# Main attention of a hybrid decoder step: the gate over the row sum goes into the rows of probabilities before they are turned, both branches add up in one PSUM bank

## The reference, cut to what matters

```python
def masked_softmax(s, mask):
    s = jnp.where(mask, s, NEG_INF)
    p = jnp.where(mask, jnp.exp(s - jnp.max(s, axis=-1, keepdims=True)), 0.0)
    return p / jnp.maximum(jnp.sum(p, axis=-1, keepdims=True), TINY)
...
    p = masked_softmax(s, (dist_s >= 0)[:, :, None])
    o_slc = jnp.einsum('bgrqk,bgqkd->bqgrd', p, vg.astype(F32))
...
    o_win = window_prompt(q, k_win, v_win, slopes)
...
    o_nsa = gate[:, :, 0, :, :, None] * o_cmp + gate[:, :, 1, :, :, None] * o_slc + gate[:, :, 2, :, :, None] * o_win
```

## Time and profile before

| | |
|---|---|
| median of 3 runs | 1355.48 us (1353.26 to 1357.56) |
| profiled execution: its span, the one time recorded of it | 1354.8 us |
| PE busy | 1298.8 us (96%) |
| DVE / ACT / POOL busy | 619.4 / 621.8 / 145.7 us |
| main attention, first scores to last spread | about 382 to 1004 us of the span |

### The profile page before, as it was taken

One profiled execution on the slowest core, in us unless ns is written; L12 is line 12 of the kernel. 1 busy time (PEld: TensorE's weight loads), 2 busy tenths in 40 slices (PEclk: granted clock), 3 DMA queues, 4 the chain that ended last, 5 costly groups with the idle time before them and its releaser, 6 DMA issues.

```text
span 1354.8 us, 23612 instructions
## 1 busy us (share of the span) xinstructions
PE 1298.8 (96%) x9533; PEld 1170.1 (86%) x9533; DVE 619.4 (46%) x1387; ACT 621.8 (46%) x1072; POOL 145.7 (11%) x184
## 2 busy tenths in 40 slices
PE   5999998999999999999999999999988989999998
PEld 4999998999988889989888889888866779999876
DVE  6211145645834343433323333466578767453342
ACT  6211336542555536666556645665467542221121
POOL 2100001103300000000000300313010260000000
PEclk9999999999999999999999999999999999899999
DMA  7251453522422211122212221554345656452331
GB/s 207 63 171 42 120 149 103 147 69 61 79 69 59 64 59 60 48 79 64 65 59 79 60 59 52 172 168 147 101 155 197 245 180 193 136 157 64 109 121 59
DMA packets 156908, 145.27 MB, mean 107 GB/s; under 512 B 27360, under 2 KB 141360, under 8 KB 156736
## 3 DMA queue, kind: packets, MB, share of 16 engines
q1 hardware_dynamic: 154016, 135.33, 33.1%
q0 software_dynamic: 2784, 8.43, 2.1%
HBM read 105.88 MB, written 41.88 MB: 109 GB/s over the span
## 4 chain that ended last, share of the span: by engine, by line
PE 56%; ACT 2%; DVE 2%; issue 1%; SPq 0%; DMA 0%; another core or an unknown queue 0%; POOL 0%; DVEq 0%; ACTq 0%
PE ps L240 31%; PE ps L2536 7%; PE ps L1645 4%; PE ps L1679 4%; PE ps L1661 3%; PE ps L1694 1%; PE ps L2443 1%; PE ps L2411 1%; DVE S L2648 1%; PE ps L2447 1%; PE ps L1764 1%; PE ps L2544 1%; PE ps L2502 0%; DMA m_raw<-in_w_branch_a 0%; SPq L3012 0%
## 5 line engine op out<-in xcount | busy, mean ns | idle before, releaser
L240 PE MATMUL ps<-hH,wH 128*128 128x352 f32 (+1 forms) x1320 | 440.0, 333 | 5.8 <-DVE stg L375 3.0
L240 PE MATMUL ps<-hH,wL 128*128 128x352 f32 (+1 forms) x1320 | 425.3, 322 | 0.0
L240 PE MATMUL ps<-hL,wH 128*128 128x352 f32 (+1 forms) x1320 | 424.8, 322 | 0.0
L240 PEld LDWEIGHTS ps<-hH,wH 128*128 128x128 f32 (+1 forms) x1320 | 248.1, 188 | 32.9 <-issue 26.5
L240 PEld LDWEIGHTS ps<-hL,wH 128*128 128x128 f32 (+1 forms) x1320 | 249.1, 189 | 2.2 <-issue 1.9
L240 PEld LDWEIGHTS ps<-hH,wL 128*128 128x128 f32 (+1 forms) x1320 | 247.8, 188 | 0.3
L227 DVE TENSOR_TENSOR wL<-w_raw,wH 128x1024 fp32r<-128x1024 f32 (+1 forms) x70 | 87.8, 1254 | 132.8 <-ACT wH L219 132.7
L2002 DVE CUSTOM_DVE_ANT_0 sP<-ps,dist,stat 128x256 f32<-128x256 f32 (+3 forms) x116 | 58.6, 542 | 176.8 <-issue 108.2
L360 ACT ACTIVATE stg<-ps 128x352 f32<-128x352 f32 x132 | 61.1, 463 | 119.1 <-PE ps L240 117.3
L219 ACT ACTIVATE wH<-w_raw 128x1024 fp32r<-128x1024 f32 (+1 forms) x70 | 73.5, 1050 | 70.5 <-issue 39.5
L2199 ACT ACTIVATE pPT<-ps 128x512 f32<-128x512 f32 x74 | 44.1, 596 | 131.9 <-PE ps L1661 131.8
(11 more groups left out here) (391 smaller groups left out, 2035.1 us busy)
## 6 DMA issues: line engine op xcount, KB each, us to landing
w_raw<-in_w_in SPq DMA_DIRECT2D x61, 512.0 KB, 4.1
p_spill<-stg SPq DMA_DIRECT2D x132, 176.0 KB, 1.8
zt<-p_spill SPq DMA_DIRECT2D x24, 528.0 KB, 4.8
w_raw<-in_w_in SPq DMA_DIRECT2D x17, 256.0 KB, 3.8
gvT<-p_spill SPq DMA_DIRECT2D x8, 528.0 KB, 5.4
x_all<-in_x_prompt SPq DMA_DIRECT2D x8, 512.0 KB, 10.0
m_raw<-in_w_branch_b SPq DMA_DIRECT2D x8, 512.0 KB, 5.5
xr<-in_x_prompt SPq DMA_DIRECT2D x8, 512.0 KB, 3.5
```

Source lines behind the costliest of these rows:

```text
L240: mm = nc.tensor.matmul(ps[0:t.m, bank, 0:NF], w[:, c % 2, t.m * k:t.m * k + t.m], x[n][:, k, :], start=(k == 0 and i == 0), stop=(k == t. ...
```

## The change

The weights go into the rows of probabilities instead of the outputs. For each row, DVE takes max and reciprocal of the two row sums, and then multiplies the whole row of `sP` in place, once for each group, with 1 / row sum and with the gate (one instruction with two factors that are columns of one value per partition). PE's turns wait for that (`weighed`) instead of for the exponentials. Since both branches then come out weighted, they add up in the same 256 columns. The spread on PE, its copy on ACT and the two additions on POOL are gone; DVE's `drain` adds 256 columns of PSUM to `oTn`. ACT's exponentials of the first 49 steps run one cut further ahead.

```diff
             def transposes(m):
...
-                    pe.wait_ge(sem("probs"), 2 * cuts[m][-1][0] + g + 1)
+                    pe.wait_ge(sem("weighed"), 2 * cuts[m][-1][0] + g + 1)
...
-                    col = P * (2 * br + i % 2)
+                    col = P * (i % 2)
...
-                                start=c + k == 0, stop=c + k == blocks_of[n] - 1)
+                                start=br == 0 and c + k == 0, stop=br == 1 and c + k == blocks_of[n] - 1)
...
                 slot(t, 3)
-                for j in closed(m - 1):
-                    spread(j)
...
+            def weigh(m):
+
+                nonlocal weighed
+                while weighed < len(U) and (last_cut(weighed) <= m + LA - 2 or cut_of[weighed, 0] <= m):
+                    n = weighed
+                    r, i, br = U[n]
+                    j = n // 4
+                    dve.wait_ge(sem("probs"), 2 * n + 2)
+                    l, w = lcol[:, j % 2, :, br, i % 2], wcol[:, j % 2, :, br, i % 2]
                     link(nc.vector.tensor_scalar(w, l, TINY, None, ALU.max))
                     link(nc.vector.reciprocal(w, w))
+                    for g in range(G):
+                        p = sP[:, g, P * spot[n]:P * (spot[n] + blocks_of[n])]
+                        col = 8 * (br + 1) + R * g + r
+                        nc.vector.tensor_scalar(p, p, wcol[:, j % 2, g, br, i % 2:i % 2 + 1], gate[:, i, col:col + 1],
+                                                ALU.mult, ALU.mult).then_inc(sem("weighed"), 1)
+                    weighed += 1
...
             def drain(j):
...
-                nc.vector.tensor_tensor(tmp[:, j % 2, :], tmp[:, j % 2, :], ps[:, 6 + j % 2, :], ALU.mult)\
-                    .then_inc(sem("O_out"), 1)
+                o = oTn[:, r, 2 * P * ip:2 * P * ip + 2 * P]
+                nc.vector.tensor_tensor(o, o, ps[:, 6 + j % 2, 0:2 * P], ALU.add).then_inc(sem("O_out"), 1)
...
             def tail_step(m):
 
                 t = m - M0
+                weigh(m)
                 slot(t, 0)
...
             for m in range(ncut):
                 if m >= M0:
                     tail_step(m)
                     continue
+                weigh(m)
                 dve_units(dve, units_at(m) - 1)
...
-            def spread(j):
-
-                act.wait_ge(sem("w_spread"), j + 1)
-                if j >= 2:
-                    act.wait_ge(sem("o_added"), j - 1)
-                copy(tmp[:, j % 2, :], ps[:, 4, :]).then_inc(sem("w_copied"), 1)
...
-                while rows < len(U) and (last_cut(rows) <= m + LA - (1 if m >= M0 else 2) or cut_of[rows, 0] <= m):
+                while rows < len(U) and (last_cut(rows) <= m + LA - 1 or cut_of[rows, 0] <= m):
```

More of the change, by code:

```diff
@@ L1110, in closed @@
             return [j for j in range(4 * R) if last_cut(4 * j + 3) == m]
-        def spread_before(m):
-            return sum(last_cut(4 * j + 3) + 1 < m for j in range(4 * R))
         def units_at(m):
@@ L1484, in turned @@
             act.wait_ge(sem("gv_done"), NV * h + p + 1)
-            if h == 0 and j < 2:
-                act.wait_ge(sem("o_added"), 4 * R - 1 + j)
-            elif h == 0:
+            if h == 0 and j >= 2:
                 act.wait_ge(sem("av_done"), ncut)
@@ L1890, in _ @@
             pool.wait_ge(sem("cmp_out"), PT)
-            add(0)
+            pool.wait_ge(sem("O_out"), 1)
             for name in cmp_sems:
                 pool.sem_clear(sem(name))
-            for j in range(1, 4 * R - 6):
-                add(j)
             first_biases()
-            add(4 * R - 6)
             pool.wait_ge(sem("u_done"), NE)
@@ L2015, in copies @@
                         drain(j)
-            def weigh(j):
-                r, ip = divmod(j, 4)
-                if j >= 2:
[L2021 to L2024, removed]
+            weighed = 0
+            def weigh(m):
[6 more added lines that the diff above has]
+                    l, w = lcol[:, j % 2, :, br, i % 2], wcol[:, j % 2, :, br, i % 2]
                     link(nc.vector.tensor_scalar(w, l, TINY, None, ALU.max))
                     link(nc.vector.reciprocal(w, w))
[L2027 to L2031, removed]
+                    for g in range(G):
[4 more added lines that the diff above has]
+                    weighed += 1
             def drain(j):
-                dve.wait_ge(sem("w_copied"), j + 1)
+                r, ip = divmod(j, 4)
+                if j == 0:
+                    dve.wait_ge(sem("cmp_out"), PT)
                 dve.wait_ge(sem("av_done"), last_cut(4 * j + 3) + 1)
-                nc.vector.tensor_tensor(tmp[:, j % 2, :], tmp[:, j % 2, :], ps[:, 6 + j % 2, :], ALU.mult)\
-                    .then_inc(sem("O_out"), 1)
+                o = oTn[:, r, 2 * P * ip:2 * P * ip + 2 * P]
+                nc.vector.tensor_tensor(o, o, ps[:, 6 + j % 2, 0:2 * P], ALU.add).then_inc(sem("O_out"), 1)
             def decode_queries():
@@ L2240, in probs @@
                 if n % 4 == 0 and j >= 2:
-                    act.wait_ge(sem("w_ready"), j - 1)
+                    act.wait_ge(sem("weighed"), 8 * (j - 1))
                 act.wait_ge(sem("scored"), 2 * (last_part[n] + 1))
@@ L2320, in _ @@
                 act_units(act, units_at(m) - 1)
-                copies(m)
+                pT_copy(m)
                 act_units(act)
```

37 lines of the change are left out of this document (3 added, 34 removed).

## The result

The changed kernel takes 1359.85 us (median of 11 runs, 1358.27 to 1364.01) against 1354.92 us (1350.22 to 1357.56): ratio 1.0033, interval 1.0021 to 1.0044. Run again in a second series it took 1359.70 us against 1355.43 us, ratio 1.0028 (1.0015 to 1.0040). So it is slower by 4 to 5 us. The forecast was 1354.6 us and no measurable change.

A forecast was written before the change was run, and what follows sets the result against it. PE's list was taken to bound the main attention; -16.5 (spreads) + 16.4 (waits) + 1.9 (weight loads) + 1.3 (slow clock) - 2.5 - 1.1 - 0.4 = -0.9 us, so 1354.6 us, with a range of 1347 to 1366.

The forecast's parts named there:

- PE's list bounds the stretch, and the spreads are worth 16.5 us: Main attention: PE busy 615.5 of 626 us; removing 16 spreads of 1.03 us takes 16.5 us off its list.
- The price of a weighing: On DVE: 0.52 ns a column, 347 ns for one weighing of 128 columns.
- The rival of full rate: DVE weighs at 1.04 ns a column, PE waits in twice as many steps: about +13, 1368 us; chance 0.16.
- The waits on the weighing: PE's turns in the main attention wait for DVE's weighed rows: 17 waits, 16.4 us in all.
- The first kind: Rows over three cuts ending a one-unit step (steps 13, 26, 46): PE waits 1.65 us each, 5.3 us in all.
- the third: Steps from 49 on, one unit each, `head_part` ahead of the weighing: 3.0 us in steps 51, 54, 55, 57, 58.
- The rival that the cover holds: DVE reaches the weighings earlier, only step 64's wait and slow clock remain: about 1345 us; chance 0.12.
- The rival of ACT holding up the units' banks: Earlier exponentials delay ACT's bank-freeing copies; PE waits in a quarter of 27 two-unit steps: +6, 1361 us; chance 0.06.
- What hangs on the waits: Behind each of 17 waits PE loads weights for 0.11 us, 1.9 us; clock effects were also counted here.
- the zb wait: PE's 2.6 us wait on a DVE product shrinks by 1.2 us and loses its 1.3 us of slow clock: -2.5.
- The clock: Slow clock costs 1.3 us more behind step 64's wait; 1.3 us of it goes behind the 2.6 us product wait.
- POOL's end: At the very end POOL's last additions hold the next stage's buffers; their removal gives -0.4 us.

The follow-up runs named there:

- Without weighing: The changed kernel with no weighing issued, PE's turns waiting for the exponentials, row sums and gates left out of the output: 1336.09 us, ratio to before 0.9846.
- the third profile of before: The kernel before the change, unedited, run and profiled a third time: 1356.34 us, ratio 1.0005, 602.12 us to cut 64.
- the filled wait: The changed kernel plus 44 additional matmuls on PE that keep it at work during its 5.5 us wait at cut 64: 1357.19 us, ratio to before 1.0016.
- the last row early: The changed kernel with the last row's weighing moved ahead in step 63, before the next stage's factors on DVE: 1355.90 us, ratio to before 1.0005.

## Why the prediction was wrong, step by step

- **PE's list bounds the stretch, and the spreads are worth 16.5 us: right, but for the last one.** The 15 spreads up to cut 64 are 15.4 us of PE. Without weighing 19.3 us go; the forecast for the same terms was 16.5 + 2.5, but 2.0 us of the 19.3 are waits that neither the forecast nor the expectation had (above).
- **The price of a weighing: right**, 344 and 810 ns. The rival of full rate is out.
- **The waits on the weighing: right in place, and in total with some luck.** 16.1 us forecast as 16.4. Steps 13, 26, 46: 1.44, 1.75, 0.95 us (1.65 each; the rows it was worked out from give 1.57); 0, 15, 40, 42: 0.75, 0.80, 0.58, 0.27 (0.85, 0.9, 0.6, 0.3); 51, 54, 55, 57, 58: 4.1 together (3.0); 64: 5.50 (5.5). The first kind came 0.8 us below, the third 1.1 above. The forecast counted 17 waits; its own list has 13 places, and 13 is what the trace shows. The rival that the cover holds is out in this order, and comes true as soon as the order is changed. The rival of ACT holding up the units' banks is out too: PE waits for no copy of a unit by ACT.
- **"What hangs on the waits": the step that failed.** It had 1.9 us of weight loads behind the waits and no more. Against the third profile of before, the stretch to cut 64 is 3.5 us longer, and neither profile has slow clock in a busy part of it. 15 spreads x 1.03 and 1.2 us of the zb wait have gone (-16.6) and 16.1 us of waits have come; 4.0 us remain. 13 weight loads of 0.14 us are 1.8 of it; the forecast's 1.9 was 17 of 0.11, a price that no row had shown. The other 2.2 us are nine waits of the weight loads of 0.17 to 0.30 us each, seven of them for a second group; I had counted 0.1 us for these in three steps.
- **The clock, part of the same step.** The forecast put its net at nothing: 1.3 us paid behind step 64, 1.3 us back at the zb wait. The credit is right on the average but not in each execution: 1.4, 2.8 and 0 us in three profiles. Behind step 64 it cost 1.7 us in the rows and 2.5 to 2.7 us by the filled wait. The mean clock of the runs, 0.993 before, 0.989 after and 0.993 with the wait filled, says that the net is a loss.
- **POOL's end: right, but a wait beside it grew.** ACT's copies of the next stage's values (vh), which POOL's additions held up, kept PE 0.7 us before and 0.3 after: the forecast -0.4. PE's wait for `drain` ahead of it grew from 0.5 to 1.1 us: the last spread, 1.0 us of PE, no longer stands between the last values and this wait, while on DVE two products of 1.26 us each still stand ahead of `drain`. So more than half of what the last spread gave was lost again. PE at the start of the next stage, before and after, and the wait on vh after:

```profile
1002.32 1.04 PE L1694 MATMUL ps<-ident,wcol 128*64 128x128 f32 x16
1004.88 1.09 PE L1360 MATMUL ps<-ident,gvT 128*128 128x128 f32 x8 [0.49 <-DVE tmp L2037]
1009.17 1.13 PE L2411 MATMUL ps<-vh,kt 128*128 128x256 f32 x4 [0.74 <-ACT vh L1490]
```
```profile
1006.67 1.09 PE L1355 MATMUL ps<-ident,gvT 128*128 128x128 f32 x8 [1.08 <-DVE oTn L2002]
```
```profile
PE ps L2356 <- ACT vh L1483: 0.3, 1, 0.3
```

- **The base.** The execution that I took every row from held 3.2 us of losses that the other two have not; the sum of differences did not use them, but they hid the 3.5 us: by its own first profile the stretch to cut 64 became 0.9 us shorter.

With the measured terms and the clock left aside: -16.5 + 16.1 + 4.0 - 1.2 - 1.1 - 0.4 + 0.6 = +1.5 us. Another 0.35 us lies outside the span (the recorded time is 1.75 us above the span for before, 2.10 for after; why is not known). That fits the +2.0 us (0.3 to 4.1) of the kernel with the wait filled, which has the mean clock of before. The slow clock adds 2.5 to 2.7 us: +4.4 to +4.6, beside +4.3 (2.0 to 5.4) in the second series and +4.9 in the first. Of the 5.3 us between this and the forecast's -0.9, the loads and second waits are 2.1, the clock 2.6, the wait for `drain` 0.6; the waits themselves and the 0.35 us outside the span nearly cancel.

## What to carry to other kernels

Work moved from the busy engine to an idle one is free only if it comes in time: find what stands ahead of it in the idle engine's list at each place where the busy one needs it. Here the same instructions were worth +4 us or -10 us by their order alone. And count a wait with what it drags along (the load behind it, the second half of a pair, the clock), and take more than one profile of the kernel before when the sum is a difference of two large terms.

## What the runs showed of the hardware

- A product of 128 columns in place with two factors per partition took DVE 344 ns; one with a single factor, not in place, took 282. How much of the difference is the second factor's is not separated here.
- The clock was 0.50 behind a wait of 5.5 us, and 1.00 with PE at work on filler. With the same four waits of 0.6 to 1.1 us it was at a mean of 1.00, 0.83 and 0.88 over 14 us in three executions of before, and 0.66 in one of the last row early; behind 2.6 us it fell to 0.50 in two profiles of three and stayed at 1.00 in the third.
- The exponential starts 0.01 to 0.02 us after its table load of 1.28 us. The Trainium skill (ScalarE: Activation LUTs, What ACT_TABLE_LOAD costs) adds a drain of about 1.38 us to each switch; no row here shows it, and moving the load took 1.28 us off PE's wait.
